# Two stages of a two-layer DeltaNet/RWKV-7 backbone reordered: the output stage begun within the scan's last steps, the key norm moved into the middle of the features

## The chip, the cores and the metric

The kernel runs on one core of a Trainium2 chip. The metric is the device time of one execution in microseconds (us). TensorE (PE) does matmuls, VectorE (DVE), ScalarE (ACT) and GpSimd (POOL) elementwise work, SyncE (SP) issues the DMAs. Each engine has a queue of its own that runs in order; engines wait for each other by semaphores.

## What is computed

A backbone of two layers over 256 context and 512 latent tokens, 1024 wide. Each layer is

```
x <- x + 1/2 * g1 * SwiGLU_1(mod1(RMSNorm(x)))
x <- x + g2 * W_out [GatedDeltaNet heads | RWKV-7 heads](mod2(RMSNorm(x)))
x <- x + 1/2 * g3 * SwiGLU_2(mod3(RMSNorm(x)))
```

The change touches two places of the RWKV-7 half (8 heads of 64 channels, so 4 tiles of 128 channels; d is the scan's direction) and the product that follows it:

```
# features
w_log = -softplus(-(w0 + tanh(lw) @ w2)) - 0.5;  a = sigmoid(a0 + la @ a2)
kk    = l2_normalize(heads(k * k_k))                 # the key norm
k_dir = k * (1.0 + (a - 1.0) * k_a)
bonus = sum(r * k_dir * u[d]) * v                    # per head, both directions
# after the scans
y     = scan_fwd + scan_bwd + bonus
yn    = (y - mean(y)) * rsqrt(var(y) + 64e-5) * weight + bias     # per head
out   = concat([deltanet, yn * (sigmoid(lg) @ g2)]) @ W_out
```

In the second layer only the latent tokens go on from W_out.

## The kernel before, in words

**Layout.** Activations lie with channels on the partitions and the 768 tokens along the free axis. One large SBUF tile, the arena, is divided by hand into regions by column; tensors whose lives don't overlap share columns. PSUM has 8 banks; `RSTD` names banks 6 and 7 from column 256 of bank 6 on. fp32 products of the dense stages are made from a high and a low part of each operand, three passes (high by high, high by low, low by high). ACT makes the high part (`split_high`, L1280, or a copy), DVE the low part by subtraction (`split_low`, L1285). `pe_product` (L1288) runs the three passes for one of 8 input tiles.

**Order of a layer.** FFN, projection and DeltaNet scan, RWKV projection, features (`*_feat`), RWKV scan (`*_rw`, 12 chunks of 64 tokens in both directions), output stage (`*_out`), second FFN. Every function is written once per engine, and the order in each is written out by hand. Semaphore values are counted as well.

**Features.** For each tile j and direction d, PE multiplies the decay and rate weights (`lora`, L2327) into PSUM banks 0 to 2 (d = 0) or 3 to 5 (d = 1); ACT makes two sigmoids of it and one factor (`gates`, L2266: L2269, L2271, L2274); DVE sums the log decays along the chunk (`scan`, L2390); POOL multiplies the factor with the keys (L2570). The bonus starts on ACT (`begin_bonus`, L2283), DVE finishes it in two operations (`bonus`, L2395: L2398 and a multiply), PE sums it over each head (`sum_bonus`, L2354) in banks 0 to 3, and DVE multiplies it with v (`take_bonus`, L2407). The key norm: ACT squares (`square`, L2277), PE sums per head (`sum_squares`, L2339), ACT takes the root (L2307, another function table than the sigmoid's), PE turns it so that tokens lie on the partitions (`pe_head_turn`, L1307), DVE inverts (L1318), ACT widens the value of a head over its channels (`widen`, L2288), PE spreads it back (`spread`, L2345) into one of two places (RSTD, or banks 4 and 5), DVE multiplies (`normalize`, L2403). The squares and their sums come in the middle; from the root on everything comes after the last gates. POOL prepares chunk 0 of the scan in the same phase: its first four multiplies need ACT's exponentials, the rest the normalized keys. `pe_hold` (L503) issues matmuls of no use on an unused place of PSUM: 14 of them stand before the scan's first matmul.

**Scan.** In every step PE, ACT and DVE pass small tiles back and forth; POOL prepares chunks ahead. ACT copies the chunk's output in `move_out` (L2807).

**Output stage.** SP loads W_out's tiles 0 and 1 (512 KB each) into a double buffer, the DeltaNet half of the mixer's result (1.5 MB, saved to DRAM earlier) and the residual stream (3 MB). It may begin only when all four engines have passed the scan (`dma_after(sp, start_of(layer, 7))`, L3192). DVE adds both directions and the bonus (`add`, L3073), PE averages per head (L3032, into two banks for each of the four tiles), DVE centers (L3078), ACT squares, PE sums squares (L3038), ACT takes the root, PE turns, DVE inverts, and for each tile j ACT widens (L2985), PE spreads (L3051) and multiplies the gate (L3054), DVE scales (L3111) and weighs (L3114, L3115), then the tile is split (high on ACT, L2980; low on DVE, L3091). The products run for output tiles 0 and 1 together (`tiles(k)`, L3021, for input tile k): k = 0 to 3 (the DeltaNet half) after the turn, each later one after its spread and gate. From output tile 2 on (L3059) each tile's eight products run in one piece, with its weights loaded, split and added to the residual in turn. PE's order:

```
averages 0..3; sums of squares 0..3; turn; tiles 0..3
spread 0, gate 0; spread 1, gate 1, tiles 4; spread 2, gate 2, tiles 5;
spread 3, gate 3, tiles 6; tiles 7; then output tiles 2 to 7
```

## Time and profile before

| | us |
|---|---|
| median of 3 runs | 4022.79 (4021.42 to 4027.47) |
| the profiled execution | 4033.49 |
| its span, first to last instruction | 4031.8 |
| granted TensorE clock, mean | 0.988 |

| engine | busy us | share of the span |
|---|---|---|
| PE | 3817.7 | 95% |
| PE weight loads | 3336.3 | 83% |
| DVE | 2206.8 | 55% |
| ACT | 1455.2 | 36% |
| POOL | 760.1 | 19% |

How to read it: one execution was profiled; its times are compared among themselves, and it was 10.7 us longer than the median of the runs. Busy shares are means over stages with very different limits. Weight loads overlap matmuls. Where a row of the timeline merges several instructions, xN says how many, and one fp32 matmul can stand as two records or more. The granted clock is 1.00 at TensorE's full 2.4 GHz and 0.50 at 1.2 GHz. POOL's spans are rough.

### The profile page before, as it was taken

How to read it: one execution, taken by the hardware profiler on the slowest of the kernel's cores; microseconds unless marked ns; L12 is line 12 of the kernel's file. 1: busy time of each engine (PE TensorE's matmuls, PEld its weight loads, DVE VectorE, ACT ScalarE, POOL GpSimd, SP SyncE). 2: the span in 40 equal slices, each digit the busy share in tenths (PEclk: the TensorE clock that was granted, in tenths of full speed). 3: DMA queues.
4: the chain of work that ended last, by engine and by line, in shares of the span. 5: the costliest groups of instructions: out<-in, count | busy, mean ns of one | idle time of the engine just before them, and what ended most of it. 6: DMA issues, size and time to landing. Idle time of an engine off the chain costs nothing. (4 is left out here: it accounts for less than half of the span.)

```text
span 4031.8 us, 93050 instructions
## 1 busy us (share of the span) xinstructions
PE 3817.7 (95%) x40211; PEld 3336.3 (83%) x40211; DVE 2206.8 (55%) x3770; ACT 1455.2 (36%) x2510; POOL 760.1 (19%) x879
## 2 busy tenths in 40 slices
PE   7999999999988888999999999999999988889999
PEld 5899998878867767999998999987887867758887
DVE  4655556466464444755556655566565464444444
ACT  4333334343353333433334333343333253333232
POOL 1222210043023310222211222200232043300000
PEclk9999999999999999999999999999999999999999
DMA  6433332100200021323223333332100200032332
GB/s 214 126 119 105 105 102 74 37 13 2 77 11 4 5 70 43 113 87 99 87 66 116 107 113 105 105 105 58 28 2 17 71 2 5 5 110 80 88 112 66
DMA packets 409036, 287.20 MB, mean 71 GB/s; under 512 B 13438, under 2 KB 366180, under 8 KB 408164
## 3 DMA queue, kind: packets, MB, share of 16 engines
q1 hardware_dynamic: 408676, 281.86, 22.9%
q8 instruction: 292, 4.78, 0.5%
q14 instruction: 68, 0.56, 0.0%
HBM read 270.27 MB, written 11.53 MB: 70 GB/s over the span
## 5 line engine op out<-in xcount | busy, mean ns | idle before, releaser
L804 ACT ACTIVATE w_hi<-w_raw 128x512 fp32r<-128x512 f32 (+1 forms) x724 | 406.0, 613 | 645.0 <-POOL w_raw L788 347.9
L811 DVE TENSOR_TENSOR w_lo<-w_raw,w_hi 128x512 fp32r<-128x512 f32 (+1 forms) x724 | 484.9, 710 | 170.7 <-ACT w_hi L804 170.7
L919 PE MATMUL PS<-x_hi,w_hi 128*128 128x384 f32 x1680 | 562.4, 335 | 1.4 <-DVE hid_flat L1106 1.4
L919 PE MATMUL PS<-x_lo,w_hi 128*128 128x384 f32 x1680 | 561.3, 334 | 0.0
L919 PE MATMUL PS<-x_hi,w_lo 128*128 128x384 f32 x1680 | 561.2, 334 | 0.0
L1191 DVE SCALAR_TENSOR_TENSOR arena<-PS,mod,arena 128x256 f32<-128x256 f32 (+1 forms) x336 | 198.4, 632 | 332.5 <-PE PS L932 332.3
L1106 DVE TENSOR_TENSOR hid_flat<-hid_flat,PS 128x384 f32<-128x384 f32 (+1 forms) x454 | 246.1, 557 | 239.5 <-PE PS L919 153.1
L932 PE MATMUL PS<-hidden_hi,w_hi 128*128 128x256 f32 (+1 forms) x1232 | 341.7, 347 | 7.7 <-DVE hidden_lo L1158 5.7
L932 PE MATMUL PS<-hidden_lo,w_hi 128*128 128x256 f32 (+1 forms) x1232 | 336.9, 343 | 0.0
L932 PE MATMUL PS<-hidden_hi,w_lo 128*128 128x256 f32 (+1 forms) x1232 | 336.7, 343 | 0.0
L781 POOL TENSOR_TENSOR w_raw<-w_raw 128x512 f32<-128x512 f32 x60 | 86.3, 1438 | 1271.1 <-DMA w_raw<-in_ffn_w_dram 1186.8
L919 PEld LDWEIGHTS PS<-x_hi,w_hi 128*128 128x128 f32 x1680 | 315.4, 188 | 2.0 <-DVE hid_flat L1106 2.0
L919 PEld LDWEIGHTS PS<-x_lo,w_hi 128*128 128x128 f32 x1680 | 315.4, 188 | 0.2
L919 PEld LDWEIGHTS PS<-x_hi,w_lo 128*128 128x128 f32 x1680 | 315.4, 188 | 0.0
L932 PEld LDWEIGHTS PS<-hidden_hi,w_hi 128*128 128x128 f32 x1232 | 228.2, 188 | 63.9 <-issue 30.6
L932 PEld LDWEIGHTS PS<-hidden_hi,w_lo 128*128 128x128 f32 x1232 | 231.4, 188 | 29.1
L932 PEld LDWEIGHTS PS<-hidden_lo,w_hi 128*128 128x128 f32 x1232 | 231.5, 188 | 28.9
L2523 POOL TENSOR_TENSOR arena<-arena 128x256 f32<-128x256 f32 (+1 forms) x240 | 170.5, 732 | 256.1 <-ACT arena L2516 256.1
L1762 PEld LDWEIGHTS PS<-arena 128*128 128x128 f32 x1344 | 155.5, 192 | 24.6 <-DVE arena L1994 10.0
L1762 PE MATMUL PS<-arena 128*128 128x128 f32 x1344 | 162.6, 278 | 12.5 <-DVE arena L1994 7.7
L1292 PE MATMUL PS<-p_hi,pw_hi 128*128 128x256 f32 (+1 forms) x544 | 142.9, 344 | 4.1 <-DVE pw_lo L1285 2.9
L1292 PE MATMUL PS<-p_hi,pw_lo 128*128 128x256 f32 (+1 forms) x544 | 138.7, 337 | 0.0
(359 smaller groups left out, 7402.1 us busy)
## 6 DMA issues: line engine op xcount, KB each, us to landing
w_raw<-in_ffn_w_dram SPq DMA_DIRECT2D x512, 256.0 KB, 4.0
arena<-in_ada_w_dram SPq DMA_DIRECT2D x120, 512.0 KB, 5.8
arena<-in_w_in_dram SPq DMA_DIRECT2D x64, 512.0 KB, 3.9
arena<-in_ada_w_dram SPq DMA_DIRECT2D x6, 2048.0 KB, 14.7
arena<-in_w_out_dram SPq DMA_DIRECT2D x16, 512.0 KB, 4.3
h_save<-arena SPq DMA_DIRECT2D x16, 384.0 KB, 2.7
arena<-h_save SPq DMA_DIRECT2D x2, 3072.0 KB, 16.6
w_raw<-in_ffn_w_dram SPq DMA_DIRECT2D x32, 128.0 KB, 2.3
```

The lines of the kernel that those rows point to most:

```text
L781: v.tensor_tensor(w[:, BOTH, :], w[:, DIFF, :], w[:, UP1, :], ALU.add).then_inc(weights_summed, 1)
L804: nc.scalar.activation(w_hi[:, high_place(n, what, j), 0:size], w_raw[:, load_of[what] % 2, place, 0:size], ACT.Copy).then_inc(w_high_read ...
L811: nc.vector.tensor_tensor(w_lo[:, b, place, 0:size], w_raw[:, b, place, 0:size], w_hi[:, high_place(n, what, j), 0:size].bitcast(F32), ALU ...
L919: mm = pe.matmul(PS[:, 4 * b + bank, 0:half], w[wo], x_split[xo][:, j, k, 0:half], start=(k == 0 and q == 0), stop=(k == KH - 1 and q == 2))
L932: mm = pe.matmul(PS[:, 2 * (k % 2) + s, 0:wd], w[wo], hid_split[xo][:, f, a0:a0 + wd], start=(f == 0 and q == 0), stop=(f == tiles - 1 and ...
L1106: v.tensor_tensor(out, x, y, op).then_inc(combined, 1)
L1191: ins = v.scalar_tensor_tensor(h[:, k, a0:a0 + w], PS[:, 2 * (k % 2) + s, 0:w], mod[:, c, at:at + 1], h[:, k, a0:a0 + w], ALU.mult, ALU.add)
L1292: mm = pe.matmul(PS[:, bank_ + s, 0:w], pw[wo][:, b, k * P:(k + 1) * P], x[xo][:, k, a:a + w], start=(k == 0 and q == 0), stop=(k == KT - ...
L1762: mm = pe.matmul(PS[:, b, u * P:(u + 1) * P], lhs[:, u, :], rhs[:, u, :], start=start and (stop or u == 0), stop=stop and (start or u == D ...
L2523: mult = lambda out_, a, b: gp.tensor_tensor(out_, a, b, ALU.mult)
```

## The change

**Places in the arena.** The directed keys and the key tensor move by 768 columns, one of the scan's working pairs and two masks move to columns below them, and the low parts of the mixer's DeltaNet half are written over the half itself, so that the first output weights (raw in columns of r, split in columns of the directed keys) and the split mixer have free columns once POOL has read its last chunk.

**Output stage.** SP waits for POOL's last copy of the layer and not for the scan's end; then it issues the loads of W_out's tiles 0 and 1 (to a region of their own), of the mixer half and of the residual. The wait for the scan's end comes after these, before tile 2; tiles 2 and 3 no longer wait for tiles 0 and 1 to be split. ACT splits weights 0 and 1 within the last full step of the scan and the first two mixer tiles within the step after it; DVE makes the four low parts right after its last scan operation. PE takes tiles 0 to 3 between the averages, uses banks 4 to 7 for the averages (two tiles at a time), and does gate 0 before the turn and spread 1 before weighing 0 ends. ACT loads the root's table before the squares.

**Features.** The root, turn, inversion and spreads are moved between gates (0,1) and gates (3,0). There is one place for spreads now. The four bonus sums come after the last gates.

```diff
 # features, ACT
-            for j in range(NB):
-                for d in range(2):
-                    gates(j, d)
-                if j == 0:
-                    square(2)
-                    square(3)
-                else:
-                    begin_bonus(j - 1)
-                if j == NB - 2:
-                    sc.activation(lora_g, lora_g, ACT.Sigmoid)
+            gates(0, 0)
+            gates(0, 1)
+            square(2)
+            square(3)
             act.wait_ge(kk_summed, K0(layer) + NB)
             sc.activation(fsq_rows, RSTD[0:8, :], ACT.Sqrt, bias=eps[0:8, 0:1]).then_inc(kk_rooted, 1)
-            begin_bonus(NB - 1)
+            gates(1, 0)
             act.wait_ge(kk_step, (1 + 2 * NB) * layer + NB + 1)
             widen(0)
             widen(1)
+            gates(1, 1)
+            begin_bonus(0)
+            gates(2, 0)
+            widen(2)
+            gates(2, 1)
+            begin_bonus(1)
+            widen(3)
+            sc.activation(lora_g, lora_g, ACT.Sigmoid)
+            gates(3, 0)
+            gates(3, 1)
+            begin_bonus(2)
+            begin_bonus(3)
...
-            widen(2)
-            widen(3)
 # features, PE
             def spread(j):
                 pe.wait_ge(kk_squared, K1(layer) + NB + j + 1)
-                if j >= 2:
-                    pe.wait_ge(kk_step, (1 + 2 * NB) * layer + NB + j)
+                if j >= 1:
+                    pe.wait_ge(kk_step, (1 + 2 * NB) * layer + NB + 1 + j)
                 for t in range(T // P):
-                    mm = pe.matmul(KK_PLACE[j % 2][:, t * P:(t + 1) * P], fsq[:, j % 2, t * P:(t + 1) * P], ident[:, :],
+                    mm = pe.matmul(RSTD[:, t * P:(t + 1) * P], fsq[:, j % 2, t * P:(t + 1) * P], ident[:, :],
                                    start=True, stop=True)
...
             lora(0, 0)
             lora(0, 1)
-            for j in range(1, NB):
-                if j < 3:
-                    sum_squares(2 * j - 2)
-                    sum_squares(2 * j - 1)
-                for d in range(2):
-                    lora(j, d)
+            sum_squares(0)
+            sum_squares(1)
+            sum_squares(2)
+            sum_squares(3)
+            lora(1, 0)
+            lora(1, 1)
             pe.wait_ge(kk_rooted, 2 * layer + 2)
             pe_head_turn(pe, fsq_rows).then_inc(qk_summed, 1)
-            sum_bonus(0)
-            sum_bonus(1)
             spread(0)
+            lora(2, 0)
             spread(1)
+            lora(2, 1)
             spread(2)
+            lora(3, 0)
             spread(3)
-            sum_bonus(2)
-            sum_bonus(3)
+            lora(3, 1)
+            pe.wait_ge(gates_ready, WAYS * (layer + 1))
+            for j in range(NB):
+                sum_bonus(j)
 # features, DVE
-            for j in range(NB):
+            for j in range(2):
                 for d in range(2):
                     scan(j, d)
-                if j > 0:
-                    bonus(j - 1)
-            dve.wait_ge(qk_summed, (layer + 1) * HEAD_STEPS)
-            dve_head_invert(dve).then_inc(kk_step, 1)
-            bonus(NB - 1)
+                if j == 0:
+                    dve.wait_ge(qk_summed, (layer + 1) * HEAD_STEPS)
+                    dve_head_invert(dve).then_inc(kk_step, 1)
+            bonus(0)
             normalize(0)
+            scan(2, 0)
             normalize(1)
+            scan(2, 1)
+            normalize(2)
+            bonus(1)
+            scan(3, 0)
+            normalize(3)
+            scan(3, 1)
+            bonus(2)
             take_bonus(0)
-            take_bonus(1)
-            normalize(2)
-            normalize(3)
-            take_bonus(2)
-            take_bonus(3)
+            bonus(3)
+            for j in range(1, NB):
+                take_bonus(j)
 # scan, ACT, the last full step (d == RW_CHUNKS - 1) and the one after it
                     move_kb(d, 0)
+                    if d == RW_CHUNKS - 1:
+                        act_out_weights(act, layer, 0)
                     move_y(d, 3)
                     move_kb(d, 1)
+                    if d == RW_CHUNKS - 1:
+                        act_out_weights(act, layer, 1)
+                else:
+                    act_out_high(act, layer, 0)
+                    act_out_high(act, layer, 1)
                 if c is not None:
                     move_out(c)
 # scan, DVE, at its end
+            for t in range(2):
+                dve_out_weights(dve, layer, t)
+            dve_out_low(dve, layer, 0)
+            dve_out_low(dve, layer, 1)
 # output, SP
+            sp.wait_ge(rw_copied, (COPIES * RW_CHUNKS + ZEROED + WAYS) * (layer + 1))
             load(0)
             load(1)
             sp.dma_start(mix_dn[:, :, :].rearrange("p a b -> p (a b)"), mix_save).then_inc(h_loaded, 16)
             sp.dma_start(h[:, :, :].rearrange("p a b -> p (a b)"), h_save).then_inc(h_saved, 16)
+            dma_after(sp, start_of(layer, 7))
             for t in range(2, KT):
+                if t >= 4:
+                    sp.wait_ge(low_split, SPLIT0 + layer * SPLITS + SPLIT_W[t - 2] + 1)
                 load(t)
 # output, ACT
+            act_out_high(act, layer, 2)
+            act_out_high(act, layer, 3)
+            act_warm(act)
+            for j in range(NB):
+                square(j)
...
 # output, PE
+            pe_out_tiles(pe, layer, 0)
+            average(0)
+            pe_out_tiles(pe, layer, 1)
+            average(1)
+            pe_out_tiles(pe, layer, 2)
+            average(2)
+            average(3)
+            pe_out_tiles(pe, layer, 3)
             pe.wait_ge(go_step, d0 + CENTERED[NB - 1])
...
+            gate(0)
             pe.wait_ge(go_act, a0 + NB + 1)
             pe_head_turn(pe, go_rows).then_inc(go_summed, 1)
...
+            spread(0)
+            spread(1)
+            gate(1)
+            spread(2)
+            gate(2)
+            pe_out_tiles(pe, layer, NB)
+            spread(3)
+            gate(3)
+            for k in range(NB + 1, KT):
+                pe_out_tiles(pe, layer, k)
 # output, DVE
             add(0)
             add(1)
             center(0)
+            dve_out_low(dve, layer, 2)
             add(2)
             center(1)
             add(3)
             center(2)
+            dve_out_low(dve, layer, 3)
             center(3)
+            dve.wait_ge(go_summed, s0 + 10)
+            dve_head_invert(dve).then_inc(go_step, 1)
+            for j in range(NB):
+                scale(j)
+                weigh(j)
                 if j > 0:
+                    dve_out_low(dve, layer, NB + j - 1)
```

`pe_out_tiles`, `act_out_weights`, `act_out_high`, `dve_out_weights` and `dve_out_low` do what `tiles`, `split` and `mix` did before, with the new places; in `scale` and `weigh` the operations are those of L3111 and of L3114 and L3115. Spread j waits for the widening and for scaling j - 1; gate j waits for weighing j - 1.

## Rows read from the trace of the kernel before

**Rows 1.** The table by windows: each engine's busy time, TensorE's granted clock, DMA share, GB/s.

```profile
1164.00:1217.00 53.00, 42.49 (x178) 25.89 (x178) 41.95 (x38) 37.74 (x47) 29.33 (x31) 0.87 0.00 0
1474.30:1535.00 60.70, 44.62 (x199) 29.86 (x199) 33.25 (x43) 18.97 (x23) 0.00 (x0) 0.92 0.34 121
...
3543.60:3600.00 56.40, 39.53 (x150) 24.41 (x151) 30.49 (x41) 17.09 (x23) 0.00 (x0) 0.91 0.34 121
```

**Rows 2.** The timeline of TensorE in layer 0's output stage: start, duration, line, [idle before].

```profile
1476.32 5.49 PE L3032 MATMUL PS<-arena,headones 128*128 128x256 f32 x8 [2.73 <-DVE arena L3076]
...
1488.56 5.32 PE L3038 MATMUL PS<-arena,pair_band 128*8 128x256 f32 x16 [1.91 <-ACT arena L2997]
...
1495.33 0.62 PE L1292 MATMUL PS<-mix_hi,pw_hi 128*128 128x256 f32 x2
...
1503.91 1.50 PE L3051 MATMUL PS<-ident,arena 128*128 128x128 f32 x12
1505.25 1.46 PE L3054 MATMUL PS<-arena 128*128 128x256 f32 x4
...
1534.97 0.59 PE L1292 MATMUL PS<-mix_hi,pw_hi 128*128 128x256 f32 x2 [0.24 <-DVE arena L3131]
```

**Rows 3.** The timeline of DVE in the same stage.

```profile
1474.31 0.96 DVE L3074 TENSOR_TENSOR arena<-arena 128x768 f32<-128x768 f32 x1 [6.91 <-ACT arena L2811]
...
1486.75 1.02 DVE L3082 SCALAR_TENSOR_TENSOR arena<-PS,arena 128x256 f32<-128x256 f32 x2 [0.79 <-PE PS L3032]
...
1505.45 1.01 DVE L3111 SCALAR_TENSOR_TENSOR arena<-arena,prm,PS 128x768 f32<-128x768 f32 x1 [7.01 <-PE PS L3051]
...
1507.22 1.07 DVE L3115 SCALAR_TENSOR_TENSOR mix_rw<-arena,prm,PS 128x512 f32<-128x512 f32 x1
...
1512.73 0.94 DVE L3091 TENSOR_TENSOR mix_lo<-mix_rw,mix_hi 128x768 fp32r<-128x768 f32 x1
```

**Rows 4.** The timeline of ACT from the scan's last step into that stage.

```profile
1461.23 0.60 ACT L2790 ACTIVATE arena<-PS 128x512 f32<-128x512 f32 x1 [0.28 <-PE PS L2643]
...
1478.68 1.06 ACT L1280 ACTIVATE pw_hi<-arena 128x1024 fp32r<-128x1024 f32 x1 [4.40 <-DMA arena<-in_w_out_dram]
...
1486.10 1.58 ACT L2980 ACTIVATE mix_hi<-mix_dn 128x768 fp32r<-128x768 f32 x2 [2.65 <-DMA mix_dn<-mix_save]
...
1496.18 1.56 ACT L2985 ACTIVATE arena<-tok_heads 128x768 f32<-128x768 f32 x2
```

**Rows 5.** The timeline of POOL, its last entry in layer 0's scan.

```profile
1440.30 1.42 POOL L2523 TENSOR_TENSOR arena<-arena 128x256 f32<-128x256 f32 x2
```

**Rows 6.** The timeline of TensorE in layer 0's features.

```profile
1179.32 4.24 PE L2335 MATMUL PS<-arena 64*128 64x512 f32 x16
...
1197.52 0.80 PE L1307 MATMUL PS<-ident,arena 8*128 8x8 f32 x6 [8.08 <-ACT arena L2307]
1198.25 4.98 PE L2359 MATMUL PS<-arena,headones 128*128 128x256 f32 x8
...
1213.74 3.39 PE L506 MATMUL PS<-ident 128*128 128x128 f32 x28
```

**Rows 7.** The timeline of ACT in layer 0's features.

```profile
1191.70 0.88 ACT L2269 ACTIVATE arena<-PS,prm 128x768 f32<-128x768 f32 x1
...
1195.28 1.28 ACT L2307 ACT_TABLE_LOAD   x1
1196.57 0.89 ACT L2307 ACTIVATE arena<-PS,eps 8x768 f32<-8x768 f32 x1
```

**Rows 8.** The timeline of DVE in layer 0's features.

```profile
1170.16 1.76 DVE L2393 TENSOR_TENSOR_SCAN arena<-keep,arena 128x768 f32<-128x768 f32 x1 [2.30 <-ACT arena L2271]
...
1191.88 2.60 DVE L2398 SCALAR_TENSOR_TENSOR arena<-arena,prm 128x768 f32<-128x768 f32 x1
```

**Rows 9.** The timeline of POOL in layer 0's features.

```profile
1191.87 1.80 POOL L2570 TENSOR_TENSOR arena<-arena 128x768 f32<-128x768 f32 x1 [1.53 <-ACT arena L2274]
```

**Rows 10.** The table by windows, one stretch inside TensorE's longest idle time.

```profile
1193.00:1196.00 3.00, 0.00 (x0) 0.00 (x0) 2.96 (x2) 2.95 (x4) 2.16 (x2) 0.50 0.00 0
```

More of the change, by code:

```diff
@@ L2968, in act_out, with square @@
             d0, s0, a0 = GO_STEP * layer, GO_SUMMED * layer, GO_ACT * layer
[L2969 to L2993 removed]
+            def square(j):
                 act.wait_ge(go_step, d0 + CENTERED[j])
@@ L3118, in dve_out @@
                                        ALU.add, ALU.mult).then_inc(go_step, 1)
+            add(0)
+            add(1)
+            center(0)
+            dve_out_low(dve, layer, 2)
+            add(2)
+            center(1)
+            add(3)
+            center(2)
+            dve_out_low(dve, layer, 3)
+            center(3)
+            dve.wait_ge(go_summed, s0 + 10)
[3 more added lines that the diff above has]
+                weigh(j)
                 if j > 0:
-                    mix(NB + j - 1)
-            mix(KT - 1)
-            split(2)
+                    dve_out_low(dve, layer, NB + j - 1)
+            dve_out_low(dve, layer, KT - 1)
+            dve_out_weights(dve, layer, 2)
             dve.wait_ge(h_saved, H_MOVES * (layer + 1))
@@ L3125, in dve_out @@
                 if 0 < t < KT - 2:
-                    split(t + 2)
+                    dve_out_weights(dve, layer, t + 2)
                 dve.wait_ge(proj_summed, 2 + layer * PT + DNB + t + 1)
-                for s, (a0, w) in enumerate(segs):
-                    at = 0 if a0 == 0 else 1
-                    hv, g = h[:, t, a0:a0 + w], mod[:, 5 * KT + t, at:at + 1]
+                for s, (a0_, w) in enumerate(segs):
+                    at = 0 if a0_ == 0 else 1
+                    hv, g = h[:, t, a0_:a0_ + w], mod[:, 5 * KT + t, at:at + 1]
                     ins = v.scalar_tensor_tensor(hv, PS[:, 2 * (t % 2) + s, 0:w], g, hv, ALU.mult, ALU.add)
```

179 lines of the change are left out of this document (88 added, 91 removed).

## The prediction

> **What bounds the kernel now.** I first cut four stretches out of the table by windows, since the change touches only two stages of each layer: the features (from the first decay matmul, 1164, to the first scan matmul, 1217) and the start of the output stage (from the scan's last output copy, 1474.3, to the first product of output tile 2, about 1535; in layer 1, 3543.6 to 3600) [rows 1]. TensorE has idle time in all of them: it is busy 42.5 of 53 us, 44.6 of 60.7 and 39.5 of 56.4, at a mean granted clock of 0.87 to 0.92. Behind the start of tile 2 come six output tiles of products back to back, so a microsecond saved before that point is a microsecond of the program.
>
> Next the timeline of TensorE in the output stage [rows 2]: idle 2.73 us before the first average, whose two tiles (eight matmuls) take 5.49 us, idle again before the pair sums, and the tile products of the saved half (from 1495.33) only behind both. DVE has the same stage as a chain [rows 3]: adds at once, then a scale (1.01) and a weighting for each tile, each behind a spread. ACT waits 4.40 us for the first output weights and gets the other group's saved tiles only at 1486.1 [rows 4]. The work it waits for needs nothing of the scan: GpSimd's last copy ends at 1440.30 + 1.42 = 1441.7 [rows 5], and 32 us pass before the loads are issued.
>
> In the features ACT sets the pace: three activations per half tile, 2.65 us (3.58 from one half's sigmoid to the table load, less 0.93 for the begun bonus between) [rows 7], and TensorE idles 8.08 us [rows 6].
>
> **Output stage, layer 0.** Counted from 1474.3. What TensorE must do before tile 2 is: eight tile pairs of 2.14 us ((1503.91 - 1495.33)/4) = 17.1; four averages, the gates' shape, about 1.4 each = 5.7; four pair sums of 5.32/4 = 1.34, 5.4; four spreads and four gates of 1.34 (1505.25 - 1503.91), 10.7; one turn, 0.5. That is 39.4 us [rows 2]; 21 us of the 60.7 are idle or half clock.
>
> Walking the new queues forward with these durations:
> - The loads go out at 1441.7. Before, issued from 1474.3 on, the first weights ended ACT's wait after 4.4 us and the saved tiles theirs after 11.8 us [rows 4], so the latter land near 1453.5, before ACT's first new wait at about 1461 and its second at 1470.7. They cost nothing.
> - In the scan's last step ACT gets two weight splits of 1.06. The first delays the copy at 1461.23 [rows 4] by 0.8 us, of which the matmul behind it hides 0.5. DVE's two low splits and two mixer splits (4.1 us) lie in the 6.9 us in which it waited after 1467.4. The two high copies on ACT (1.6 us) end before the last output copy may start. **Cost 0.3.**
> - Adds, centers and two low splits fill DVE without a gap: eight of 0.93, four of 0.96, two of 0.88, so the last center ends at 1487.8, as now (1486.75 + 1.02) [rows 3]. Under them TensorE runs tiles 0 to 3, 8.6 us that used to stand behind the turn. Tile 3 ends at 1489.0, 0.4 after the present start of the pair sums (1488.56). Sums 5.4, gate 0 1.34 in place of the wait for the root, turn: 1496.2.
> - Invert 0.38, widening 0.78 [rows 4], spread 1.36: the first scale starts at 1499.1, not 1505.45 [rows 3].
> - From there DVE sets the pace: scale 1.0, weighting 1.46, low split 0.88 per tile plus 0.3 to 0.8 waited on a spread or a gate. The last weighting ends at 1512.4, the last low split at 1514.2, half of tile 7 at 1516.5, its add of 1.1 lets tile 2 begin at **1517.8, not 1534.97: 17.2 us less**. The same walk through the old queues gives 1532.5; the missing 2.5 us are the half-clock matmuls.
>
> **Layer 1** has 512 of 768 columns, so tile pairs of 1.4 us; everything of the norm stays. The walk gives 3583.1 against 3600: **16.9 less** (old queues by the same walk 3594; 6 us were half clock and starts).
> Weight load 2 and 3 now wait only for the scan's end, then go as before; the rest of SP's queue keeps its place. The second address range of the low tiles and the moved keys add no instruction. The extra ScalarE table load before the squares (1.28 [rows 7]) stands where ACT waits for the first center: nothing.
> Unknown: half clock in the new stage, between 0 and what the old one lost (2.5 and 6); its worst gaps are 1.4 and 1.2 us around the first spread, so I take 1.0 per layer. DMA traffic during the scan: no row shows the scan under load; the centers at 1486.75 keep 1.02 us for two with the loads of 1474 still under way, so 0; at most 1 us; traffic alone can't gain. **Sum, both layers: -17.2 - 16.9 + 0.6 + 2.0 = -31.5** (bounds -34.1 to -22).
>
> **Features.** The key norm moves from the end into the middle. It takes ACT's wait for the inverse out of the end and lets GpSimd's first chunk find its keys ready. It adds:
> - a second table switch, 1.28 us. Root, both switches (3.4 us) and 0.5 us of waiting for sum 3 put gates (1,0) at 1179.2; the two widenings put the end of (1,1) at 1185.9.
> - a place on TensorE: only one bank pair holds spreads now, so spread(1) waits for normalize(0), and the matmuls of gates (2,1) are queued behind it. DVE reaches normalize(0) only after scan (1,1), 1.76 [rows 8], and bonus(0), two instructions of which the first is shut out by a GpSimd multiply: an operation of about 0.9 takes 2.60 beside GpSimd's 1.80 begun at the same moment [rows 8, 9]. So 1185.9 + 1.7 + 2.6 + 0.9 + 0.9 = 1192.1; spread 1.4, decay and rate matmuls 2.1 (4.24/2 [rows 6]): ACT resumes at 1195.8 after 4.7 us idle.
> - Then (2,1), bonus, widening, sigmoid, (3,0), (3,1): rates of the last half at 1205.6 against 1193.4 now (1191.70 and two activations) [rows 7].
> - All four bonus sums are at the end. DVE: last scan to 1208.0, bonus(2) shut out again to 1212.3, take(0), bonus(3) to 1216.1, take(1) 1217.1; sum(3) 1218.5; hold of 3.3 us [rows 6]: scan matmuls at **1221.8**. The same walk through the old queues gives 1217.75 (trace 1213.74 + 3.39 = 1217.1). **+4.05 per layer.**
> - Clock. Before, 8.08 us of idle took TensorE from 2.4 to 1.2 GHz; it was still there at 1193 to 1196 with no work [rows 10], and eight bonus-sum matmuls then took 4.98 us [rows 6], not about 2.7. Old cover: ACT and DVE were late anyway. New idle stretches are 5.3 us (1187 to 1192) and 5.0 us (1208 to 1213), each followed by matmuls that others wait for: 3.5 us, then two sums and the hold, 6.0 us. Bounds: 0, and all 9.5 us doubled. Matmuls behind the second run partly beside DVE, and full clock returned during the work, so I take a third: **+3.2 per layer**. Features: 2 x 7.25 = **+14.5**.
>
> On the table load: in this trace the root starts 1.29 us after its load does [rows 7]. The Trainium skill ("ScalarE: Activation LUTs", What ACT_TABLE_LOAD costs) adds a drain of about 1.38 us to each switch; no such gap shows here. By it the sum would be 2.8 us dearer. The Trainium skill ("TensorE: Matmul & The Clock Gate", HAM oscillation) warns that a queue which waits between bursts pays for its clock at every burst. That is the case against this feature order.
>
> **Sum:** -31.5 + 14.5 = -17.0. The profiled execution would go from 4033.5 to 4016.5; the median of the runs is 10.7 lower and moves alike, 4022.8 to **4006**.
>
> **Rivals.**
> - Clock holds in the features: only +8.1. -31.5 + 8.1 = -23.4, 3999. For it: gaps shorter than 8.08. Against: the clock was already at 0.50 within 1193 to 1196.
> - The output stage gives less: half clock as before (8.5 instead of 2) and weight splits that hold ACT back in the scan step by some 2 us a layer: -31.5 + 6.5 + 4 = -21; features at +20, 2.8 us a layer above the forecast: -1, 4022. Against: no gap above 1.4 us.
> - Slower. Place: spreads 1 to 3 at the head of TensorE's queue. If each waits for a whole bonus shut out on both instructions (2 x 2.6), not just the first, that is 15.6 us more per layer: 14.5 + 31.2 - 31.5 = +14, 4037. It decides from 20 us of loss per layer on, that is a feature stage above 73 us. Against: DVE has only a scan before normalize(1) and (2).
> - The change doesn't do what it says: the early loads land after 1461, or the tile products don't get ahead since low splits 0 and 1 are late; ACT's wait then stops the scan. Output gain near nothing, features as forecast: 4030. Landing times leave 7 us and more.
>
> **Numbers.** Forecast 0.60, clock holds 0.17, less from the output 0.13, slower 0.05, not as it says 0.05. About 0.2%, 8 us, is what a measurement of this kernel can tell. First case and second are faster: 0.80 with a little of the third; the rest of the third is "same", with the near edge of the first: 0.14; slower 0.06. Range: forecast with its bounds, down to the clock case less 3 and up near the third: 3996 to 4018.
>
> **What would show it.** Output stage: product of tile 2 some 43.5 and 39.5 us after the scan's last output copy (now 60.7 and 56.4); the first tile product before the first average, no wait on output weights in ACT; scan end moved by under 1 us. Features: 57 to 63 us to the first scan matmul, a TensorE idle of about 5 us before spread(1), ACT idle as long before gates (2,1). I am wrong if the feature stage stays within 54 us, or if tile products wait for a low split before 1480.

## The result and the profile after

The changed kernel takes 4046.19 us (median of 5 runs, 4029.25 to 4057.76) against 4022.79 before: ratio 1.0046, interval 1.0028 to 1.0064. It is **slower by about 0.5%**; the forecast was 4006 us with a range of 3996 to 4018. The profiled execution took 4057.76 us (span 4056.0) against 4033.49 (4031.8), so 24.2 us of span are to be explained. Both profiled executions are long ones of their kernels, 11.6 and 10.7 us above the medians.

First the table by windows of the changed kernel: features of layer 0, output stage of layers 0 and 1 (answering to [rows 1]), then in each layer the last full step of the scan, from one pair of output copies on ACT to the next.

```profile
1163.70:1233.40 69.70, 57.68 (x178) 32.56 (x178) 37.56 (x38) 39.23 (x48) 31.82 (x31) 0.73 0.00 0
1494.90:1539.40 44.50, 40.29 (x197) 27.38 (x196) 29.23 (x39) 15.85 (x20) 0.00 (x0) 1.00 0.12 32
3583.60:3624.00 40.40, 34.48 (x149) 21.35 (x147) 27.04 (x37) 14.27 (x19) 0.00 (x0) 1.00 0.10 26
...
1456.90:1484.30 27.40, 22.12 (x739) 19.60 (x731) 9.60 (x24) 8.78 (x16) 0.26 (x1) 0.88 0.57 214
3545.30:3573.50 28.20, 21.28 (x733) 18.72 (x726) 9.60 (x24) 8.79 (x16) 0.23 (x1) 0.88 0.56 208
```

The same step in the kernel before:

```profile
1441.80:1462.80 21.00, 18.59 (x722) 16.43 (x714) 9.60 (x24) 7.00 (x13) 0.00 (x0) 1.00 0.02 5
3512.40:3532.90 20.50, 18.34 (x716) 16.26 (x709) 9.60 (x24) 6.97 (x14) 0.00 (x0) 1.00 0.02 5
```

Three things are to be seen. The output stage fell from 60.7 to 44.6 us and from 56.4 to 40.5, at full clock, close to the 43.5 and 39.5 of the forecast. The features, here and below from the first weight load of the decay matmuls to the first scan matmul, grew from 53.1 to 69.8 us (and from 52.5 to 72.2 in layer 1), at a mean clock of 0.73 where it had been 0.87. And a scan step that the change was not to touch grew from 21.0 to 27.3 and from 20.5 to 28.2 us, with DMA busy for over half of it (before 0.02) and at a mean clock of 0.88 (before 1.00).

The sum over the span, after less before: output stage -16.1 and -15.8 (each to the first product of tile 2), features +16.6 and +19.8, whole scan +4.2 and +7.9 (its other steps vary by a few us between executions), all else +7.6. Together +24.2. The +7.6 lie in the long stretch from tile 2 of layer 0 to layer 1's features, 1710.3 us rather than 1702.6, where the clock was halved for 37.5 us rather than 17.1. The kernels of the experiments take 1698 to 1706 us for it, 1702.4 with this output stage alone and 1702.1 with these features alone, so nothing shows that it comes from the change.

TensorE in layer 0's output stage, changed kernel, answering to [rows 2]:

```profile
1494.42 0.59 PE L3034 MATMUL PS<-mix_hi,pw_hi 128*128 128x256 f32 x2 [0.27 <-issue]
...
1496.89 1.56 PE L3101 MATMUL PS<-arena,headones 128*128 128x256 f32 x4
...
1509.68 5.33 PE L3127 MATMUL PS<-arena,pair_band 128*8 128x256 f32 x16
...
1518.39 1.61 PE L3111 MATMUL PS<-ident,arena 128*128 128x128 f32 x12 [1.42 <-ACT arena L3060]
...
1521.19 1.57 PE L3111 MATMUL PS<-ident,arena 128*128 128x128 f32 x12 [1.20 <-DVE arena L3170]
...
1539.42 0.59 PE L3034 MATMUL PS<-mix_hi,pw_hi 128*128 128x256 f32 x2 [0.35 <-DVE arena L3208]
```

The first tile product stands ahead of the first average, and the largest gaps are the two around the first spread, 1.42 and 1.20 us. This part did what it says.

TensorE in layer 0's features, answering to [rows 6]:

```profile
1174.27 5.29 PE L2349 MATMUL PS<-arena,pair_band 128*8 128x256 f32 x8 [3.67 <-ACT arena L2284]
1179.48 4.55 PE L2342 MATMUL PS<-arena 64*128 64x512 f32 x16
...
1186.21 2.27 PE L2357 MATMUL PS<-ident,arena 128*128 128x128 f32 x12 [1.71 <-ACT arena L2294]
1188.41 5.49 PE L2342 MATMUL PS<-arena 64*128 64x512 f32 x8
1194.67 2.90 PE L2357 MATMUL PS<-ident,arena 128*128 128x128 f32 x12 [0.78 <-DVE arena L2393]
1197.50 5.48 PE L2342 MATMUL PS<-arena 64*128 64x512 f32 x8
...
1214.05 2.94 PE L2342 MATMUL PS<-arena 64*128 64x512 f32 x8
...
1225.00 2.90 PE L2366 MATMUL PS<-arena,headones 128*128 128x256 f32 x4 [3.38 <-DVE arena L2420]
```

and ACT beside it, answering to [rows 7]:

```profile
1193.93 0.90 ACT L2272 ACTIVATE arena<-PS,prm 128x768 f32<-128x768 f32 x1 [3.59 <-PE PS L2342]
...
1203.03 0.90 ACT L2272 ACTIVATE arena<-PS,prm 128x768 f32<-128x768 f32 x1 [5.61 <-PE PS L2342]
...
1211.30 0.90 ACT L2272 ACTIVATE arena<-PS,prm 128x768 f32<-128x768 f32 x1 [3.23 <-PE PS L2342]
```

The decay and rate matmuls of one direction alone (L2342 x8) take 5.49 us here, where the forecast reckoned 2.1; ACT, which used to set the pace, waits for each of them. The clock in that stretch and in its twin of layer 1:

```profile
1187.20:1214.00 26.80, 26.02 (x66) 16.40 (x65) 14.70 (x11) 14.24 (x17) 7.78 (x4) 0.50 0.00 1
3272.70:3299.60 26.90, 26.36 (x69) 16.92 (x68) 14.46 (x11) 14.34 (x17) 8.07 (x4) 0.50 0.00 1
```

TensorE ran at 1.2 GHz for 27 us on end although it was busy in 26 of them.

In the scan's step the timeline of TensorE has one long gap per layer, which no other engine's work ended:

```profile
1466.84 0.69 PE L2701 MATMUL PS<-arena 64*64 64x64 f32 x6 [4.24 <-issue]
...
3554.82 1.76 PE L2701 MATMUL PS<-arena 64*64 64x64 f32 x29 [4.34 <-issue]
```

The gap is not new, it is longer. The kernel before has it among the same matmuls, without any load beside it:

```profile
1448.30 0.38 PE L2686 MATMUL PS<-arena 64*64 64x64 f32 x5 [0.86 <-issue]
...
3518.41 0.97 PE L2686 MATMUL PS<-arena 64*64 64x64 f32 x26 [1.05 <-issue]
```

Nor is it all of the loss. Its growth is 3.4 us in layer 0 (4.24 less 0.86) and 3.3 in layer 1, of 6.3 and 7.7 for the step. TensorE's clock was at 1.2 GHz for 6.8 us in each layer as well, nearly all of it after the gap in layer 0, from within the gap on in layer 1:

```profile
1467.00:1473.50 6.50, 6.50 (x135) 5.86 (x139) 0.91 (x3) 2.39 (x4) 0.00 (x0) 0.50 0.99 424
3554.00:3559.20 5.20, 4.38 (x68) 3.92 (x68) 0.00 (x0) 1.79 (x3) 0.00 (x0) 0.50 1.08 459
```

SP's queue issued the early loads 7 to 10 us before TensorE's work went on in layer 0:

```profile
1457.19 1.52 SPq L2980 DMA_DIRECT2D arena<-in_w_out_dram  x2
1458.76 0.58 SPq L2985 DMA_DIRECT2D mix_dn<-mix_save  x1
1459.38 0.43 SPq L2986 DMA_DIRECT2D arena<-h_save  x1
```

The DMA view of that step names the queue that brings instructions (q8) beside the loads (q1):

```profile
q1 hardware_dynamic: 2368, 5.77, 56.1%
q8 instruction: 6, 0.10, 1.4%
```

Six packets of 16 KB, as in the 21 us of before. The view does not say whose instructions they are. Their number goes with TensorE's: in the kernel before, 65 packets beside 8382 matmuls and as many weight loads from 1210 to 1470, and 16 beside 2111 of each from 700 to 900. These are the starts of the instruction packets in layer 0, in us, from the trace's DMA records:

```
before   1434.6 1438.5 1442.2 1445.8 1449.4 1453.3 1457.2 1460.9
after    1446.7 1450.0 1453.6 1457.4 1464.5 1470.8 1474.2 1477.8
```

Before, one comes every 3.6 to 3.9 us. After, the first that falls into the loads comes 7.1 us after its forerunner and the next 6.3. TensorE stands still from 1462.6 to 1466.84, and works again 2.3 us after the late packet of 1464.5 has begun.

### The profile page after: what moved, and what is told of

The parts are those of the page before. It is cut to its first block and busy times, and to the rows that moved or that the text cites. A ratio compares the mean times of both kernels' runs of the same rounds, so it can differ in the third digit from the quotient of the medians.

```text
span 4056.0 us, 93062 instructions
## 1 busy us (share of the span) xinstructions
PE 3860.3 (95%) x40211; PEld 3360.0 (83%) x40211; DVE 2195.4 (54%) x3770; ACT 1457.0 (36%) x2514; POOL 761.9 (19%) x879
## 3 DMA queue, kind: packets, MB, share of 16 engines
q1 hardware_dynamic: 408676, 281.86, 22.7%
## 5 line engine op out<-in xcount | busy, mean ns | idle before, releaser
L1765 PEld LDWEIGHTS PS<-arena 128*128 128x128 f32 x1344 | 157.1, 193 | 24.6 <-DVE arena L1997 10.1
L1295 PE MATMUL PS<-p_lo,pw_hi 128*128 128x256 f32 (+1 forms) x544 | 138.9, 337 | 0.0
```

Source lines behind the costliest of these rows:

```text
L1295: mm = pe.matmul(PS[:, bank_ + s, 0:w], pw[wo][:, b, k * P:(k + 1) * P], x[xo][:, k, a:a + w], start=(k == 0 and q == 0), stop=(k == KT - ...
L1765: mm = pe.matmul(PS[:, b, u * P:(u + 1) * P], lhs[:, u, :], rhs[:, u, :], start=start and (stop or u == 0), stop=stop and (start or u == D ...
```

## The experiments

**Theory:** (A) the features lose by lone half-height matmuls and a halved clock; (B) the early loads delay instruction packets, and TensorE runs dry. **Rivals:** the order of the work itself, on VectorE and ScalarE (the forecast's own reading); and the new work in the scan's last step rather than the traffic. One table first, from the profiled executions (us, layer 0 / layer 1; output stage from the end of the last output copy to the first product of tile 2), then each run.

| kernel | features | last full scan step | output stage | median, its before |
|---|---|---|---|---|
| before | 53.1 / 52.5 | 21.0 / 20.5 | 60.7 / 56.4 | 4022.8 |
| changed | 69.8 / 72.2 | 27.3 / 28.2 | 44.6 / 40.5 | 4046.2, 4022.8 |
| output alone | 52.5 / 56.4 | 28.3 / 26.6 | 44.5 / 40.5 | 4013.2, 4027.4 |
| features alone | 68.6 / 64.1 | 21.1 / 20.3 | 59.6 / 53.5 | 4061.7, 4027.4 |
| pairs | 59.0 / 58.9 | 28.1 / 28.8 | 46.9 / 40.5 | 4026.9, 4027.4 |
| fillers | 59.4 / 59.4 | 28.2 / 27.9 | 44.5 / 43.0 | 4031.9, 4027.4 |
| pairs and fillers | 56.2 / 56.2 | 29.0 / 27.5 | 47.0 / 40.5 | 4020.7, 4024.8 |
| output alone, splits behind the scan | 56.4 / 56.4 | 27.3 / 25.8 | 51.5 / 48.4 | 4020.9, 4022.9 |
| output alone, residual late | 53.1 / 54.8 | 26.0 / 26.1 | 44.5 / 40.5 | 4005.2, 4024.8 |
| the same, fillers in the features of before | 54.8 / 53.1 | 25.2 / 25.1 | 44.5 / 40.6 | 4009.5, 4024.8 |
| output alone, residual late, loads one at a time | 52.5 / 53.1 | 22.7 / 21.6 | 44.5 / 42.9 | **3999.5**, 4022.9 |
| before, residual early | 52.5 / 52.5 | 24.6 / 24.4 | 61.0 / 52.3 | 4030.6, 4024.8 |
| before, residual early in pieces | 52.5 / 54.8 | 20.8 / 21.6 | 61.7 / 52.1 | 4027.7, 4022.9 |
| all together | 57.8 / 57.9 | 22.3 / 21.9 | 44.5 / 43.0 | 4010.8, 4022.9 |

### The two parts alone

Output stage, places and loads of the changed kernel, feature functions of before; and the reverse:

```diff
 # output alone, PE (and so for ACT and DVE): the feature functions of before
-            lora(0, 0)
-            lora(0, 1)
-            sum_squares(0)
...
+            lora(0, 0)
+            lora(0, 1)
+            for j in range(1, NB):
+                if j < 3:
+                    sum_squares(2 * j - 2)
+                    sum_squares(2 * j - 1)
+                for d in range(2):
+                    lora(j, d)
...
```

> The changed output stage with the features of before. Theory (features lose 36 us by a halved clock and lone half-height matmuls, early loads stretch the scan by 4 to 8 us a layer): output stage 44 and 40 us, features 53 and 52 us as before, a stall of about 4.3 us of TensorE in each layer's scan while the early loads run, time 4023 - 32 + 10 = about 4001 us, between 3995 and 4008. Rival one (the scan's loss comes from the halved clock that the new features leave behind, not from the loads): no stall in the scan, 4023 - 32 = 3991 us. Rival two (the early loads cost as much as they bring): 4020 us or more.

> The changed features with the output stage of before. Theory: features 70 and 72 us rather than 53 and 52, scan as before (257 and 254 us, no TensorE stall above 2 us in its last steps), time 4023 + 36 = about 4058 us, between 4050 and 4064. Rival (the features lose only about 8 us a layer and the rest of the loss is the scan's and the output stage's): 4038 us or less. Rival (the stall in the scan has nothing to do with the loads): a stall of about 4 us stands in the scan here too.

Output alone: 4013.17 us, ratio 0.9963 (0.9947 to 0.998). Features alone: 4061.7, ratio 1.0096 (1.0079 to 1.0113). The parts add up: -14.2 + 34.3 = +20, against +18.5 for both by the ratio (1.0046, interval +11 to +26), +23 by the medians. The stretched scan step stands where the early loads are and not where they aren't. The same features code can take different times, though: layer 1 takes 64.1 us in the features-alone trace, at the low clock for 20.5 us of them, where the changed kernel had 72.2 with 44.4. Output alone brought less than the theory's 4001 (3995 to 4008). The run with the features alone has the old output stage untouched, and it takes 59.6 and 53.5 us there; the trace of before happened to have 56.4 for layer 1. Against that trace the gain is 28 us, not 32, and 10 (whole scan) to 13 (last full step) go to the scan.

### Features: pairs, fillers, both

```diff
 # pairs, PE
             spread(0)
             lora(2, 0)
-            spread(1)
             lora(2, 1)
+            spread(1)
             spread(2)
             lora(3, 0)
-            spread(3)
             lora(3, 1)
+            spread(3)
 # fillers, PE: matmuls of 128 columns whose result nobody reads
+            pe_hold(pe, 6, 8)
             sum_squares(0)
...
+            pe_hold(pe, 5, 10)
             spread(1)
```

> The changed kernel, but with both half-height decay and rate groups of a tile issued side by side, (2,0) with (2,1) ahead of the second spread and (3,0) with (3,1) ahead of the fourth. Theory (a lone group of 64 rows takes 2.9 us at full and 5.5 us at half clock, two side by side 4.24 and about 8): the features fall from 69.7 and 72.2 by some 4 to 8 us each, because two groups that ran alone now overlap and more work stands before the wait; time 4046 - 12 = about 4034 us. Rival (the features are paced by VectorE's and ScalarE's chain, the form of the matmuls is covered): features within 2 us of 70, time 4043 us or more.

> The changed kernel with filler matmuls (128 columns each) in the waits of TensorE in the features: 8 ahead of the sums of squares, 10 ahead of the second spread, 4 each ahead of the third and fourth, 12 and 14 around the first two bonus sums. Theory (most of the loss beyond the 4 us of the new order is the halved clock): the 27 us at half clock in each layer's features vanish or fall below 10, the features take 58 to 61 us rather than 70 and 72, time 4046 - 22 = about 4024 us, between 4016 and 4032. Rival (the loss is the place on TensorE and VectorE's chain, at either clock): the granted clock rises but the features still take 66 us or more, time 4038 us or more.

Pairs: 4026.85, ratio 1.0004 (0.9993 to 1.0016), 7 us better than expected, with the features 10.8 and 13.3 us shorter where 4 to 8 were expected. Fillers: 4031.91, ratio 1.0010 (1.0000 to 1.0019), 8 us short of what was expected. Some 5 of these are the kernel before itself, which stood at 4027.4 beside these runs and at 4022.8 beside the changed kernel; the rest of this miss is not told, and by the same measure the pairs did 12 us better than expected, not 7. The stage does what the theory says: the clock holds, and the stage takes 59.4 us in both layers.

```profile
1162.70:1222.00 59.30, 53.76 (x285) 37.08 (x285) 37.58 (x38) 39.24 (x48) 32.60 (x31) 0.97 0.00 1
```

Each remedy alone takes off 10 us or more in either layer, so in part they act on the same thing. Layer 0's features are at the low clock for 37.5 us in the changed kernel, for 17.1 with the pairs and for 3.4 with the fillers. Why lone groups go with a low clock is not shown. The run with both:

```diff
 # pairs and fillers, PE
+            pe.wait_ge(gates_ready, WAYS * layer + 3)
+            pe_hold(pe, 2, 6)
             spread(0)
             lora(2, 0)
+            lora(2, 1)
             spread(1)
-            lora(2, 1)
...
```

> The changed kernel with both remedies for its features: the half-height groups side by side and the fillers in the waits. Theory (the order of work alone costs about 4 us a layer, as forecast, lone groups some 3 and the halved clock the rest): features 56 to 58 us, against 59 with either remedy alone and 53 before; time about 4022 us. Rival (59 us is the floor of the new order, paced by VectorE and ScalarE; each remedy alone already reaches it): features 58.5 to 60, time about 4028 us.

4020.71, ratio 0.9989 (0.9978 to 1.0000); features 56.2 us, clock 1.00 throughout. Its timeline shows a pair of groups, and behind it a wait of the kind for which the forecast looked, 2.69 us where it had some 5:

```profile
1183.94 4.24 PE L2342 MATMUL PS<-arena 64*128 64x512 f32 x16
1190.87 1.57 PE L2357 MATMUL PS<-ident,arena 128*128 128x128 f32 x12 [2.69 <-DVE arena L2403]
```

and that of the fillers run a lone group at full clock:

```profile
1192.27 2.84 PE L2342 MATMUL PS<-arena 64*128 64x512 f32 x8
```

So 16 records of both row halves take 4.24 us and 8 of one half take 2.84: they overlap when they stand together. In layer 0, then: order +3.1 (56.2 - 53.1), lone groups +3.2 (59.4 - 56.2), halved clock +10.4 (69.8 - 59.4). Only the first stands by itself. Taken the other way, pairs before fillers, the pairs bring 10.8 (69.8 - 59.0) and the fillers 2.8: 3.2 is what lone groups cost at full clock, and the rest of the 13.6 they and the low clock cost together.

A miss belongs here. With 22 fillers in the wait of 8.08 us ahead of the turn, in the features of before:

```diff
 # features of before, PE
+            pe.wait_ge(gates_ready, WAYS * (layer + 1) - 1)
+            pe_hold(pe, 2, 12)
+            pe.wait_ge(gates_ready, WAYS * (layer + 1))
+            pe_hold(pe, 5, 10)
             pe.wait_ge(kk_rooted, 2 * layer + 2)
             pe_head_turn(pe, fsq_rows).then_inc(qk_summed, 1)
```

> As the run with the residual loaded after the scan, and in the features of before 22 filler matmuls (128 columns) in TensorE's 8 us wait ahead of the head turn. Theory (that wait halves the clock, so that eight bonus sums take 4.98 us and not 2.7): features 50 to 51 us rather than 53, two layers, time 4005 - 4 = about 4001 us. Rival (behind the wait ScalarE and VectorE are late anyway, the fillers gain nothing): features 52 to 53, 4005 us.

4009.54, ratio 0.9958 (0.9942 to 0.9974), against 0.9951 without: nothing gained. The features took 54.8 and 53.1 us; a pair of groups now fell to the low clock just ahead of the fillers (5.48 us at 1183.89), and the spreads waited 2.82 us for ACT's widening all the same.

### Scan: traffic or work

The kernel before with one edit, the 3 MB of the residual loaded where the changed kernel starts its loads:

```diff
 # before, SP
+            sp.wait_ge(rw_copied, (COPIES * RW_CHUNKS + ZEROED + WAYS) * (layer + 1))
+            sp.dma_start(h[:, :, :].rearrange("p a b -> p (a b)"), h_save).then_inc(h_saved, 16)
+            dma_after(sp, start_of(layer, 7))
             load(0)
             load(1)
             sp.dma_start(mix_dn[:, :, :].rearrange("p a b -> p (a b)"), mix_save).then_inc(h_loaded, 16)
-            sp.dma_start(h[:, :, :].rearrange("p a b -> p (a b)"), h_save).then_inc(h_saved, 16)
...
-                dma_after(sp, start_of(layer, 7))
                 sp_out(sp, layer)
```

> The kernel before, with one edit: the 3 MB residual load is issued where the changed kernel issues its loads (after GpSimd's last scan copy) instead of after the scan; all else as before. Theory (traffic alone starves TensorE of instructions): a stall of TensorE for nothing but issue of 2 us or more in each layer's last scan steps, the scan 3 to 6 us longer per layer, time 4027 + 6 to 10 less up to 2 us for the weights that no longer share the queue = about 4033 us. Rival (traffic is harmless, the new work in the last step is what costs): scan within 1 us of before, time 4023 to 4029 us.

4030.6, ratio 1.0013 (1.0003 to 1.0023): traffic alone makes the old kernel slower, by little more than the interval, and its last full step 3.6 and 3.8 us longer. TensorE's timeline:

```profile
1446.08 0.58 PE L2686 MATMUL PS<-arena 64*64 64x64 f32 x5 [3.33 <-issue]
...
3517.28 1.55 PE L2686 MATMUL PS<-arena 64*64 64x64 f32 x26 [3.52 <-issue]
```

One instruction packet in each layer is late (6.3 and 6.4 us after its forerunner, the others 3.4 to 4.8), one long gap each, and the clock fell to 1.2 GHz behind it here too (0.50 from 1446.0 to 1452.0). The other way round, all 5.6 MB early but ScalarE's splits behind the scan:

```diff
 # output alone, ACT
                     move_kb(d, 0)
-                    if d == RW_CHUNKS - 1:
-                        act_out_weights(act, layer, 0)
                     move_y(d, 3)
...
+            act_out_weights(act, layer, 0)
+            act_out_weights(act, layer, 1)
+            for k in range(NB):
+                act_out_high(act, layer, k)
             act_warm(act)
```

> The kernel with the features of before and the changed output stage (5.6 MB loaded during the scan), but ScalarE's two weight splits and two mixer copies moved out of the scan's last step to behind it. Theory (the loads alone stretch the last steps, by the late instruction fetches): the last three steps still take 36 to 38 us against 31 to 32 before; the output stage 3 to 5 us longer than 44.9 and 40.9. Rival (the splits in the last step cost what the run with the residual load alone did not show, 1.5 to 3 us): 34.5 us or less, as in that run.

4020.85, ratio 0.9994 (0.9982 to 1.0005). The last full step still takes 27.3 and 25.8 us (with the splits 28.3 and 26.6), the last three together 37.5 and 36.1: the splits cost 1 us of it or less, the loads the rest. The output stage pays for their new place, 51.5 and 48.4 us.

Less traffic, then paced traffic:

```diff
 # output alone, residual late, SP
-            sp.dma_start(h[:, :, :].rearrange("p a b -> p (a b)"), h_save).then_inc(h_saved, 16)
             dma_after(sp, start_of(layer, 7))
+            load(2)
+            load(3)
+            sp.dma_start(h[:, :, :].rearrange("p a b -> p (a b)"), h_save).then_inc(h_saved, 16)
 # the same, loads one at a time, SP
             load(0)
+            sp.wait_ge(win_landed[0], 16 * (layer * (KT // 2 + (DNB + 1) // 2) + (DNB + 1) // 2 + 1))
             load(1)
+            sp.wait_ge(win_landed[1], 16 * (layer * (KT // 2 + DNB // 2) + DNB // 2 + 1))
-            sp.dma_start(mix_dn[:, :, :].rearrange("p a b -> p (a b)"), mix_save).then_inc(h_loaded, 16)
+            for u in range(NB):
+                sp.dma_start(mix_dn[:, u, :], mix_save[:, u * T:(u + 1) * T]).then_inc(h_loaded, 16)
+                if u < NB - 1:
+                    sp.wait_ge(h_loaded, 128 * layer + 64 + 16 * (u + 1))
```

> Features of before, changed output stage, but of the 5.6 MB that it loads during the scan only the first two weight tiles and the saved tiles of the other group (2.6 MB) stay there; the 3 MB of the residual come after the scan, behind output weights 2 and 3. Theory (the scan's last steps are stretched by about 7 us a layer because TensorE's instruction fetches queue behind these loads): fewer fetches are late, the two steps that grew from 21 to 28 us take 23 to 25, time 4013 - 8 = about 4005 us (4000 to 4009). Rival one (it is the weight splits and copies put into the last step, not the traffic): scan as in the changed kernel (260 us or more), 4013 us. Rival two (the residual now comes late and the stages behind wait for it): scan shorter but the output stage longer, 4012 us or more.

> As the run with the residual loaded after the scan, but its 2.6 MB of early loads go one at a time: each weight tile and each quarter of the saved tiles (384 to 512 KB) is issued only when the one before has landed. Theory (a fetch waits behind all that is queued on its DMA engine): no engine holds more than 32 KB ahead of a fetch, the fetch is late by under 1.5 us and not by 3, the TensorE stall of 3.5 to 3.9 us falls below 1.5, the last three steps take 32 to 34 us and not 35.4 to 36.6; time 4005 - 5 = about 4000 us. Rival (the delay is one of a few descriptors taken in advance, whatever is queued, or several small loads each hit a fetch): stalls of 2 us or more stay, 4004 us or more.

4005.16, ratio 0.9951 (0.9936 to 0.9967), and 3999.47, ratio 0.9939 (0.9925 to 0.9952). With 2.6 MB at once the stalls are 3.88 and 3.52 us and the step takes 26 us. One load at a time, the same 2.6 MB:

```profile
1441.94 0.38 PE L2689 MATMUL PS<-arena 64*64 64x64 f32 x5 [0.86 <-issue]
...
3497.37 1.03 PE L2689 MATMUL PS<-arena 64*64 64x64 f32 x27 [1.05 <-issue]
```

```profile
1434.90:1457.60 22.70, 19.03 (x734) 16.76 (x726) 9.59 (x24) 8.64 (x15) 0.16 (x1) 1.00 0.43 120
3491.50:3513.10 21.60, 19.09 (x732) 16.92 (x724) 9.93 (x26) 8.64 (x16) 0.26 (x1) 1.00 0.43 126
```

The mean DMA share is still 0.43, the gaps at this place are those of the kernel before (0.86 and 1.05 us; the largest anywhere in the step is 1.06), the clock stays at 1.00, and the step is back at 22.7 and 21.6 us. So the amount moved does not by itself delay the packets. By the whole time the two runs are not told apart, since their intervals overlap; the step and the gaps tell them apart. The same with the kernel before, its residual in eight pieces:

> The kernel before with the residual loaded during the scan, as in the earlier run, but in eight pieces of 384 KB, each issued when the last has landed. Theory (queue depth): the stalls of 3.33 and 3.52 us fall below 1.2 us, the last three steps take 31 to 32.5 us and not 34.3, time about 4024 us. Rival (any load hits the fetch that falls into it): more than one stall, together 3 us or more per layer, 4030 us or more.

The stage says yes: largest gaps 0.86 and 1.60 us (3.33 and 3.52 unpaced), steps 20.8 and 21.6 us, full clock.

```profile
1436.60:1457.40 20.80, 18.46 (x723) 16.43 (x718) 9.60 (x24) 7.02 (x14) 0.20 (x1) 1.00 0.41 117
3508.60:3530.20 21.60, 18.34 (x702) 16.18 (x696) 9.59 (x24) 7.00 (x13) 0.15 (x1) 1.00 0.41 114
```

The time says less: 4027.67, ratio 1.0009 (1.0000 to 1.0019), not the 4024 expected, and not to be told from the unpaced 1.0013. Why an early, paced residual does not bring the old kernel back to its own time stays open.

One rival is left untested. The paced runs differ from the others in two things: each load waits for the one before, and the large loads are cut into pieces of 384 KB. With the cut the packets on the data queue became small as well. In the last full step of layer 0, residual early and then in pieces:

```profile
q1 hardware_dynamic: 144, 3.15, 32.2%
q1 hardware_dynamic: 850, 2.33, 39.4%
```

No run cuts without waiting or waits without cutting. And the amount queued says little by itself: with 2.6 or 3 MB at once, the longest interval between instruction packets is 5.6 to 7.0 us in a layer, even where the 3 MB are a single load; with 5.6 MB it is 6.3 to 8.3, and most often a second packet is late too. So more data make more packets late, hardly one packet later; the size of a single load explains that as well as the depth of the queue does.

### All together

> The changed kernel with every remedy so far: half-height groups side by side and fillers in its features, early loads one at a time, the residual after the scan. Theory (the change's loss is these two mechanisms and nothing else; what then remains of the new feature order is 3 us a layer): features 56 to 57 us, the last full scan step 21.5 to 23 us, output stage 44.5 and 40.5 us; time that of the paced run with the features of before plus 6 us, about 4006 us (4000 to 4010). Rival (something else in the changed kernel still costs): 4014 us or more.

The changed kernel with pairs, fillers, loads one at a time and the residual after the scan: 4010.78, ratio 0.9971 (0.9957 to 0.9986), 35 us less than the changed kernel. In its profile the features take 57.8 and 57.9 us, the last full step 22.3 and 21.9, the output stage 44.5 and 43.0. It is 5 us above the expected 4006 and just outside the stated 4000 to 4010: with the features at 57.8 rather than 56.2 some 3 of them are told, the rest is inside the spread of its runs (4002.75 to 4021.36). The fastest version is the paced one with the features of before, 3999.5 us.

## Why the prediction was wrong

- **Output stage: right, with some luck in the sum.** -17.2 and -16.9 forecast, -16.1 and -15.8 measured. The walk was some 1 us too short in each layer, and the 1.0 taken for a half clock did not come, which evened it out. But the profiled execution of before was a long one in layer 1's stage, and the gain against the old stage in another trace is some 28, not 32. "The median moves alike" did not hold for that part.
- **DMA traffic during the scan: the first step that failed.** The forecast took 0, with 1 us as its bound (the lower end of its gains, -22, should read -23 by its own terms; nothing hangs on it), from rows that show centers on VectorE beside loads [rows 3]. Those rows could not answer: they price a VectorE instruction, while the scan's step is 720 small matmuls fed by a 16 KB packet every 3.7 us. Measured: +6.3 and +7.7 us for the step in the changed kernel, 3.4 and 3.3 of them the longer gap, the rest where the clock was halved. That the loads would wait for nothing and land in time was right; who would wait behind them was not asked. The Trainium skill ("DMA: Bandwidth & Descriptors", Queues, rings and completion order) says that each DMA engine turns between its queues only when a whole packet of descriptors is through (a group of transfers, not a packet of this profile). The late packets behind large loads, and punctual ones behind pieces of 384 and 512 KB, agree with it; no run shows a single engine's turns.
- **Order of the features: right in size.** +4.05 forecast, +3.1 measured with the clock held and the groups paired. The wait for normalize(0) is smaller than in the walk: 2.69 us before spread(1) in that run and 0.78 in the changed kernel, where some 5 were expected; the lone group ahead of it took 5.49 us and not 2.1.
- **"Decay and rate matmuls 2.1 (4.24/2)": mis-sized.** Half of a pair is not the price of one. Alone it takes 2.84 us at full clock and 5.49 at half; this cost +3.2 in layer 0 at full clock.
- **The clock term: mis-sized, and its bound too low.** +3.2 taken, 9.5 the bound, +10.4 and +12.8 measured by the fillers (69.8 and 72.2 less 59.4), in part shared with the lone groups. The forecast doubled the matmuls behind two idle gaps of 5 us. In the trace the clock fell behind shorter gaps (3.67 and 1.71 us), and stayed low through 27 us in which TensorE was busy, so the work there ran at half clock, not only what follows a gap. The Trainium skill's warning that was set beside the sum ("TensorE: Matmul & The Clock Gate", HAM oscillation: a queue that waits between bursts pays for its clock at each) was the better guide in sign; it speaks of waits, and the trace shows the low clock lasting through work.
- **The slower rival** had the right sign and the wrong mechanism: its price was the bonus shut out on VectorE, and it wanted a feature stage above 73 us. It was 69.8 and 72.2, and the scan gave the remaining 12.

Measured in place of the forecast, for the profiled span: output stage -31.9, features +36.4, scan +12.1, all else +7.6, together +24.2 instead of -17.0. Of the forecast's own signs, the output stage's time, its first tile product and ACT without a wait on weights were there. The scan's end (moved by 4.2 and 7.9 us, not by under 1), the feature stage (57 to 63 us expected) and the idle before spread(1) (about 5 us expected) were not.

## What to carry over

Before a transfer is moved under other work, ask which engine there consumes instructions fastest, not only which one reads the data: look at the instruction queue's packets in the DMA view, and issue bulk loads in small pieces, one at a time. Count a stall of TensorE together with the low clock behind it. When small matmuls are pulled apart and set between dependent steps of a chain, price each of them alone and at the low clock, since the old order gave both the pair's duration and the full clock. Set the profiled run against several others, stage by stage, before a gain is taken from it.

## What was not expected of the hardware

- 2.6 to 5.6 MB queued at once in large loads put up to 8.3 us between two 16 KB instruction packets instead of 3.7 and stopped TensorE for 2.4 to 5.2 us in each layer (4.24 and 4.34 in the changed kernel). The clock was at 1.2 GHz for 3.4 to 13.7 us around or behind the stop, in all but one of the layers. The same 2.6 MB in smaller loads one at a time, at a mean DMA share of 0.43, left the gaps at about 1 us, as without any load, and the clock at 2.4 GHz.
- TensorE stayed at 1.2 GHz through 26.8 us of which it was busy 26.0, with lone 64-row matmuls and spreads between them; with the same work paired the low stretches of the features were 6.8, 6.8 and 3.4 us.
- Sixteen records on rows 0 to 63 and 64 to 127 take 4.24 us together, eight on one half alone 2.84: side by side they save a quarter of 2 x 2.84. The Trainium skill ("TensorEngine Tiling (Array Packing)", Key Properties) says that different tiles run in parallel; the trace agrees, though for these fp32 matmuls it shows far less than a factor of two.
